# The last down pieces by token blocks, with the transposes inside, in a two-layer diffusion backbone

## Time and profile before

| | us |
|---|---|
| median of 3 runs (1637.95 to 1641.86) | 1638.42 |
| the profiled execution | 1642.74 |
| its span | 1641.2 |
| busy: TensorE, VectorE, ScalarE | 1598.5, 1124.8, 933.4 |
| mean granted clock of TensorE | 0.991 |

### The profile page before, as it was taken

The page is one execution under the profiler, slowest core; times in us unless marked ns, Lnnn a source line. Parts: engine busy times, 40 slices in busy tenths (PEclk is TensorE's granted clock), DMA queues, the critical chain, the costliest instruction groups (busy, mean ns, idle before and its releaser), DMA issues.

```text
span 1641.2 us, 22638 instructions
## 1 busy us (share of the span) xinstructions
PE 1598.5 (97%) x8278; PEld 1301.2 (79%) x8278; DVE 1124.8 (69%) x1478; ACT 933.4 (57%) x1347; POOL 48.8 (3%) x70
## 2 busy tenths in 40 slices
PE   7999999999999999899989999999999999999997
PEld 3886588988888887689678888888888888888885
DVE  5444533657553333543758999999999999899997
ACT  4415433622221322632667787787877787777875
POOL 0000000400000000000101000000000000000000
PEclk9999999999999999999999999999999999999999
DMA  8622732797442322542246999999999999999982
GB/s 345 216 77 103 308 127 85 264 363 239 165 169 103 116 90 103 194 182 77 65 177 269 421 420 420 382 400 379 374 388 361 391 370 401 362 393 376 372 334 73
DMA packets 68730, 428.88 MB, mean 261 GB/s; under 512 B 8880, under 2 KB 12720, under 8 KB 20656
## 3 DMA queue, kind: packets, MB, share of 16 engines
q1 hardware_dynamic: 60000, 396.93, 62.5%
q0 software_dynamic: 8656, 30.96, 5.1%
HBM read 404.25 MB, written 23.61 MB: 261 GB/s over the span
## 4 chain that ended last, share of the span: by engine, by line
PE 91%; DVE 4%; ACT 3%; DMA 1%; issue 1%; SPq 0%; DVEq 0%; ACTq 0%
PE ps L2027 28%; PE ps L2029 27%; PE ps L2028 27%; PE ps L2089 1%; PE ps L2045 1%; PE ps L2596 1%; DMA raw<-in_w 1%; DVE small L1452 1%; PE ps L2265 1%; PE ps L2286 1%; DVE raw L1668 1%; DVE wl L1198 0%; DVE raw L1667 0%; PE ps L2558 0%; PE ps L2290 0%
## 5 line engine op out<-in xcount | busy, mean ns | idle before, releaser
L1840 DVE TENSOR_TENSOR wl<-raw,wh 128x1024 fp32r<-128x1024 f32 x522 | 615.3, 1222 | 59.2 <-ACT wh L1099 52.2
L1099 ACT ACTIVATE wh<-raw 128x1024 fp32r<-128x1024 f32 x522 | 524.8, 1057 | 93.0 <-PE ps L2029 93.0
L2027 PE MATMUL ps<-wh,ah 128*128 128x512 f32 (+1 forms) x864 | 330.1, 382 | 0.5
L2029 PE MATMUL ps<-wh,al 128*128 128x512 f32 (+1 forms) x864 | 321.2, 372 | 0.0
L2028 PE MATMUL ps<-wl,ah 128*128 128x512 f32 (+1 forms) x864 | 320.5, 371 | 0.0
L2027 PE MATMUL ps<-ah,wh 128*128 128x512 f32 (+1 forms) x802 | 290.0, 362 | 6.6 <-DVE al L1228 4.7
L2029 PE MATMUL ps<-ah,wl 128*128 128x512 f32 (+1 forms) x802 | 282.2, 352 | 0.0
L2028 PE MATMUL ps<-al,wh 128*128 128x512 f32 (+1 forms) x802 | 282.1, 352 | 0.0
L2027 PE MATMUL ps<-wh,sh 128*128 128x512 f32 x536 | 209.9, 392 | 1.5 <-DVE sl L1557 1.5
L2029 PE MATMUL ps<-wh,sl 128*128 128x512 f32 x536 | 209.1, 390 | 0.0
L2028 PE MATMUL ps<-wl,sh 128*128 128x512 f32 x536 | 208.5, 389 | 0.0
(11 more groups left out here) (314 smaller groups left out, 1221.5 us busy)
## 6 DMA issues: line engine op xcount, KB each, us to landing
raw<-in_w SPq DMA_DIRECT2D x372, 1024.0 KB, 6.8
sent<-raw POOLq DMA_DIRECT2D x16, 512.0 KB, 24.5
back<-raw POOLq DMA_DIRECT2D x16, 512.0 KB, 25.2
x<-sent POOLq DMA_DIRECT2D x7, 512.0 KB, 11.0
back<-x POOLq DMA_DIRECT2D x7, 512.0 KB
x<-in_x SPq DMA_DIRECT2D x2, 1024.0 KB, 8.9
raw<-in_ukv SPq DMA_DIRECT2D x1, 1024.0 KB, 7.9
ah<-flat_rows POOLq DMA_DIRECT2D x2, 512.0 KB, 6.4
```

Of the source, the lines that this page charges most:

```text
L1099: act.activation(wh[:, J % SPLITS, piece_half(h)], slot(J % SLOTS)[:, piece_half(h)], ACT.Copy).then_inc(w_hi, 1)
L1840: ins = dve.tensor_tensor(wl[:, J % SPLITS, piece_half(h)], slot(J % SLOTS)[:, piece_half(h)], wh[:, J % SPLITS, piece_half(h)].bitcast(F3 ...
L2027: pe.matmul(out, lh, rh, start=start, stop=False)
L2029: return pe.matmul(out, ll, rh, start=False, stop=stop)
```

## The change

The hidden chunks 18 to 21 (four, before two) run by blocks of tokens. Chunks 20 and 21 are kept in `ah` and `al`, chunks 0 and 1, which are free then. The first two pairs of transposes stand inside block 3, between its chunks 19 and 20. Of the eight turned chunks, VectorE now makes 2, 3, 6 and 7 (in four buffers), ScalarE the others. Modulation pieces 40 and 41 move into piece 0, to chunk 3, and 42, 43 and 44 to chunks 4, 5 and 6. The split of OIN's piece 1, the squares of block 3 and the copy of modulation rows (`rows(10)`) come after the turned chunks on ScalarE, and the split after the gates of block 3 on VectorE. Both squares of a block run one behind the other, and the gate passes follow them. At the attention's end, the last head sum moves behind the four units of the Fourier chunks in the first token piece, and the roots of the first two sums come one unit and a half earlier. The diff, cut to its core:

```diff
@@ views
+        turned_at = lambda k: tmp[k % 2][:, 0:TL] if k // 2 % 2 == 0 else area(8704 + k % 2 * TL, TL)
+        late = NF - 2
+        hid_hi = lambda f: sh[:, f % 2, :] if f < late else ah[:, f - late, :]
+        hid_lo = lambda f: sl[:, f % 2, :] if f < late else al[:, f - late, :]
@@ scalar
             def hidden_hi(f):
-                if f >= 2:
+                if 2 <= f < late:
...
-            for d in range(NF // 2):
+            for d in range(NF // 2 - 1):
                 split(M_DOWN + d + 2)
                 if d + 1 < NF // 2:
                     hidden_hi(2 * d + 2)
                     hidden_hi(2 * d + 3)
...
-                    act.activation(junk[:, 0:512], ps[:, b, :], ACT.Square, accum_out=y_ss[:, t, 0:1]).then_inc(sem("row_sq"), 1)
-                    act.wait_ge(sem("y2_gated"), 2 * t + 1)
-                    act.activation(junk[:, 512:1024], ps[:, b + 1, :], ACT.Square, accum_out=y_ss[:, t, 1:2]).then_inc(sem("row_sq"), 1)
+                    for c in range(2):
+                        act.activation(junk[:, c * 512:(c + 1) * 512], ps[:, b + c, :], ACT.Square, accum_out=y_ss[:, t, c:c + 1]
+                                       ).then_inc(sem("row_sq"), 1)
...
             row_square("y", 2)
             for k in range(KD):
-                turned_chunk(k)
-                if k == 1:
-                    row_square("y", 3)
-                if k == 4:
-                    rows(10)
+                if k // 2 % 2 == 0:
+                    turned_chunk(k)
+                turned_hi(k)
+            split(M_OIN + 1)
+            row_square("y", 3)
+            rows(10)
             row_root("y", 2)
...
                 if u % 4 == 1 and u > 4:
                     head_squares(u // 4 - 1)
+                if u == len(ounits) - 3:
+                    head_ln(0)
+                    head_exp(0)
+                    head_ln(1)
                 if u == len(ounits) - 2:
-                    head_root(0, 1)
+                    head_exp(1)
...
             for h in range(DH):
-                if h == 2:
-                    head_root(DH // 2 - 1)
+                if h == 3:
+                    head_ln(2)
+                    head_exp(2)
@@ vector
-            for d in range(NF // 2):
+            for d in range(NF // 2 - 1):
...
-                for c in (1, 0):
-                    if c == 0:
-                        dve.wait_ge(sem("row_sq"), 2 * t + 1)
+                for c in range(2):
+                    dve.wait_ge(sem("row_sq"), 2 * t + c + 1)
...
             new_rows(1)
-            gated_rows(2)
             scaled(0)
             scaled(1)
+            gated_rows(2)
+            for k in range(0, KD, 4):
+                turned_chunk(k + 2)
+                turned_low(k)
+                turned_chunk(k + 3)
+                for n in range(1, 4):
+                    turned_low(k + n)
             gated_rows(3)
-            for k in range(KD):
-                low(N_O1L, k)
+            split(M_OIN + 1)
             new_rows(2)
             new_rows(3)
             split(M_OIN + 2)
@@ tensor
                 order = [(t, k) for k in (6, 7, 0, 1, 2, 3, 4, 5) for t in range(2)] if p == 0 else [(t, k) for t in range(2) for k in range(KD)]
                 for n, (t, k) in enumerate(order):
+                    if p == 0 and n == 4:
+                        head_sums(DH // 2 - 1)
...
-            for f in range(NF - 2):
+            for f in range(NF - 4):
...
             pe.wait_ge(w_lo, M_DOWN + NF // 2)
             pe.wait_ge(sem("hid_lo"), NF)
-            for t in range(ROW_BLOCKS):
-                for f in (NF - 2, NF - 1):
-                    mm = down_rows(f, t)
-                mm.then_inc(sem("y2_ps") if t < ROW_BLOCKS - 1 else w_used, 1)
...
+            for t in range(ROW_BLOCKS):
+                for f in range(NF - 4, NF):
+                    if (t, f) == (ROW_BLOCKS - 1, NF - 2):
+                        pe.wait_ge(sem("tok_made"), 2)
+                        for j in range(2):
+                            turn_pair(N_O1L, j)
+                    mm = down_rows(f, t)
+                    if (t, f) == (ROW_BLOCKS - 1, NF - 3):
+                        mm.then_inc(w_used, 1)
+                mm.then_inc(sem("y2_ps") if t < ROW_BLOCKS - 1 else w_used, 1)
             pe.wait_ge(sem("row_sq"), 2)
             pe.wait_ge(sem("y2_gated"), 2)
-            mod_piece(GAP_MODS)
-            mod_piece(GAP_MODS + 1)
-            pe.wait_ge(sem("tok_made"), 2)
-            for j in range(2):
-                turn_pair(N_O1L, j)
...
             def latent_chunk(k):
-                if k in (2, 4):
-                    pe.wait_ge(mod_h, MOD_H_BEFORE[N_O1L] + k)
-                    turn_pair(N_O1L, k // 2 + 1)
+                if k == 1:
+                    pe.wait_ge(mod_h, MOD_H_BEFORE[N_O1L] + 2)
+                    turn_pair(N_O1L, 2)
+                if k == 2:
+                    pe.wait_ge(sem("turned_dve"), 2)
+                    turn_pair(N_O1L, 3)
+                for n in {3: (0, 1), 4: (2,), 5: (3,), 6: (4,)}.get(k, ()):
+                    mod_piece(GAP_MODS + n)
                 pe.wait_ge(mod_lo, MOD_BEFORE[N_O1L] + k + 1)
-                if k in (1, 3, 5):
-                    filler(GAP_MODS + 2 + k // 2)
...
             for p in range(OIN):
+                if p == 1:
+                    pe.wait_ge(sem("y2_gated"), 2 * ROW_BLOCKS)
...
-            pe.wait_ge(sem("diff_out"), len(ounits))
-            head_sums(DH // 2 - 1)
             for p in range(4):
                 token_piece(p)
```

More of the change, by code:

```diff
@@ L177 @@
 MOD_BEFORE = {N_E1: 0, N_E2L: KD, N_E2C: 2 * KD, N_O1L: 3 * KD, N_O1C: 4 * KD}
-MOD_H_BEFORE = {N_E2L: KD, N_E2C: 2 * KD, N_O1L: 3 * KD, N_O1C: 4 * KD}
+MOD_H_BEFORE = {N_E2L: KD, N_E2C: 2 * KD, N_O1L: 3 * KD, N_O1C: 3 * KD + KD // 2}
 def cols_of(n):
@@ L850, in hidden_hi @@
                 act.wait_ge(evac_dve, evacs(hidden_evac(f), "dve"))
-                act.activation(sh[:, f % 2, :], hid[:, f, :], ACT.Copy).then_inc(sem("hid_hi"), 1)
+                act.activation(hid_hi(f), hid[:, f, :], ACT.Copy).then_inc(sem("hid_hi"), 1)
             for m in range(3, NF):
@@ L901, in row_root, with turned_bank, turned_hi @@
                 act.activation(col, col, ACT.Exp, scale=-0.5).then_inc(sem("row_root"), 1)
+            def turned_bank(k):
+                return ps[:, 4 + k // 2 % 2, (k % 2) * TL:(k % 2 + 1) * TL]
             def turned_chunk(k):
                 act.wait_ge(sem("tok_ps"), pair_ps(N_O1L, k // 2))
[L906 to L912, removed]
+                if k >= 4:
+                    act.wait_ge(mod_lo, MOD_BEFORE[N_O1L] + k - 3)
+                act.activation(turned_at(k), turned_bank(k), ACT.Identity, bias=mod1[:, k, 0:1], scale=scl[:, 1, 0, k, 0:1]).then_inc(mod_h, 1)
+                act.wait_ge(mod_h, MOD_H_BEFORE[N_O1L] + 2 * (k // 4) + k % 2 + 1)
+            def turned_hi(k):
+                if k // 2 % 2:
+                    act.wait_ge(sem("turned_dve"), 2 * (k // 4) + k % 2 + 1)
+                act.activation(ah[:, k, 0:TL], turned_at(k), ACT.Copy).then_inc(mod_hi, 1)
             def context_hi(k):
@@ L1004, in head_squares, with head_ln, head_exp @@
                 act.activation(two_heads(o_sq, n), two_heads(o_o, n), ACT.Square).then_inc(sem("osq_ready"), 1)
[L1006 to L1014, removed]
+            def head_ln(n):
+                act.wait_ge(sem("ossq_done"), n + 1)
+                act.activation(two_heads(o_rinv, n), ps[:, HEAD_SUMS[n], :], ACT.Ln, bias=eps[:, 0:1], scale=1.0 / P
+                               ).then_inc(sem("oln"), 1)
+            def head_exp(n):
+                act.wait_ge(sem("oln"), n + 1)
+                act.activation(two_heads(o_rinv, n), two_heads(o_rinv, n), ACT.Exp, scale=-0.5).then_inc(sem("oroot"), 1)
             attention("diff", ounits, exp_o, out_o, last_piece)
@@ L1556, in hidden_lo @@
                 dve.wait_ge(sem("hid_hi"), f + 1)
-                dve.tensor_tensor(sl[:, f % 2, :], hid[:, f, :], sh[:, f % 2, :].bitcast(F32), ALU.subtract
+                dve.tensor_tensor(hid_lo(f), hid[:, f, :], hid_hi(f).bitcast(F32), ALU.subtract
                                   ).then_inc(sem("hid_lo"), 1)
@@ L1605, in scaled, with turned_chunk, turned_low @@
                                   ).then_inc(sem("tok_made"), 1)
+            def turned_chunk(k):
+                dve.wait_ge(sem("tok_ps"), pair_ps(N_O1L, k // 2))
+                if k >= 4:
+                    dve.wait_ge(mod_lo, MOD_BEFORE[N_O1L] + k - 3)
+                dve.tensor_scalar(turned_at(k), ps[:, 4 + k // 2 % 2, (k % 2) * TL:(k % 2 + 1) * TL],
+                                  scl[:, 1, 0, k, 0:1], mod1[:, k, 0:1], ALU.mult, ALU.add).then_inc(sem("turned_dve"), 1)
+            def turned_low(k):
+                dve.wait_ge(mod_hi, MOD_BEFORE[N_O1L] + k + 1)
+                dve.tensor_tensor(al[:, k, 0:TL], turned_at(k), ah[:, k, 0:TL].bitcast(F32), ALU.subtract).then_inc(mod_lo, 1)
```

(9 more changed lines are left out.)

## The result

The changed kernel takes 1654.97 us (median of 4 runs, 1652.61 to 1656.47) against 1638.59: a ratio of 1.009, 95% interval 1.0076 to 1.0104, so 16.4 us slower. Its profiled execution took 1656.47 us, span 1654.8, against 1642.74 and 1641.2: 13.7 us more.

A forecast was written before the change was run, and what follows sets the result against it. The prediction took TensorE's gaps and clock to bound the kernel. 10.4 us lost up to modulation 46 less 3.1 gained at the attention's end gave +7.3; with 0.8 more on the median 1638.42 this made 1646.5 us, range 1641 to 1651.

The forecast's parts named there:

- The wait ahead of the blocks: Before the last four hidden chunks, TensorE idles 5.35 us: a loss of 3.8, plus 2.4 for the low clock.
- Piece 0 starts without a wait: Second layer's first projection: TensorE starts piece 0 at the down product's end, where before it waited 3.29 us.
- The split moved past a queue: Inside piece 0, OIN piece 1's split ends at E + 10.5, modulation 42 lands at E + 15.3, TensorE stands 9.7 us.
- part 3: From piece 0 to modulation 46: the late split delays the fetches, so 46 starts at 707.3, 10.4 us later.
- it lands near 25.4; 1.8 idle: Modulation 45, fetched behind OIN's piece 2 in turns of 2.6 us, lands near E + 25.4; TensorE idles 1.8.
- now 46 is early enough, 7.46: From modulation 45's start to 46's: 7.46 us, where the kernel before took 8.05 with 0.59 idle.
- the low clock through the broken piece: Rival, chance 0.10: the low clock stays through piece 0's alternating work and waits, 4.5 us more, 1651.
- Part 4: Attention's end: head sums behind the Fourier chunks, first token piece ends 3.1 us earlier, bounds 1.0 and 4.2.
- I added 0.8: Added to the median 1638.42 because quicker runs may partly lack the low-clock stretches removed; half of the 1.7 us.
- the covered case: Bound of the fetch term: with the fetch covered entirely, piece 0 ends at E + 11.9, modulation 46 starts 2.5 us earlier.

The follow-up runs named there:

- Taking its cause out: Changed kernel with hidden chunks 20 and 21 split ahead of 18 and 19, all four ahead of the split of OIN's piece 0: 1.0041 of the kernel before.
- all causes out: Changed kernel with hidden chunks 20 and 21 first, OIN piece 1's split ahead of all turned chunks, modulation 45 behind piece 1: 0.9961 and 0.9965 of before in two runs.
- the kernel with TensorE kept busy: Changed kernel with modulation 45 behind piece 1, plus 19 unread matmuls in the gap before modulation 42: 1.0052 of the kernel before.
- Part 4 alone: The kernel before with only the head-sum edits of the diff: 0.998 of the kernel before, some 3.3 us faster.
- The three causes: Taken out of the changed kernel singly: hidden chunks 20 and 21 first, 1.0041; OIN piece 1's split between turned chunks 3 and 4, 1.0031; modulation 45 behind piece 1, 1.0058.
- the kernel with separate buffers: The kernel before with the head-sum edits and hidden chunks 20 and 21 kept in ah and al: 0.9974 of the kernel before.

## Why the prediction was half right

The direction and the chain of causes were right; the size was too small: +8 forecast, +16.4 measured, outside the range, which ended at 1651.

- *The wait ahead of the blocks.* 5.35 forecast, 5.36 in the trace; resumed at 649.15 against 649.32, and the down product's end E at 674.4 in both. Taking its cause out gave 8 us, uncertain by some 3, where 3.8 + 2.4 = 6.2 were booked.
- *Piece 0 starts without a wait.* Right.
- *The split moved past a queue.* Issue at E + 10.5 forecast, E + 10.4 measured (684.80); landing 4.7 us later; the gap 9.7 against 9.19. Moving the split gave back 9.7 us, uncertain by some 3.
- *The step that failed* is in the sum of part 3: "it lands near 25.4; 1.8 idle" for modulation 45, and behind it "now 46 is early enough, 7.46". I gave each queued fetch a turn of 2.6 us, from the one pair in the earlier trace rows. With several under way, 44 landed 10.4 us after its issue at 685.6 (at 696.0, 1.1 later than forecast), OIN 2 after 7.0 (698.6) and 45 after 7.5 (702.5): 6.5 us for the last two, 3.2 each. So 45 started at 702.55 and not at 699.8 (2.8 us). The wait for 45 was 3.80 us, and that brought the clock down a third time: from 45 to 46 it took 10.26 and not 7.46 (2.8 us). Together 5.5 of the 8.3 us that were missed. The trace of before had shown that 2.6 isn't the turn of every queued fetch: the piece that SyncE issued at 698.16, behind three other fetches (1.6 MB) in the 1.3 us before, landed 9.2 us later. The forecast named this as a rival, the low clock through the broken piece, with 0.10 and 4.5 us; it came true in part, through piece 1 and not through piece 0, and should have had the larger share. The Trainium skill's section on HAM oscillation (TensorE: Matmul & The Clock Gate) says that bursts between waits for data start at the low clock each time. The trace agrees for the waits of 9.19 and 3.80 us on the DMA (0.50 in the windows), and the wait of 5.36 on VectorE did the same; waits of 1.20 and 1.99 us in the first run with all causes out left the clock whole. The section counts half of the low stretch as lost. Behind 45 this stretch lasts until about 709.0, 6.4 us, so half would be 3.2, and 2.8 is near it: matmuls of 256 columns go from 0.12 to 0.21 us apart there, not to 0.24. In piece 0, however, the kernel with TensorE kept busy shows a price near nothing.
- *Part 4.* 3.1 forecast. In the changed kernel's trace the first transposes of the next stage come 12.4 us late (870.88 against 858.45), 15.9 less 12.4 = 3.5; alone it gave 3.3. The working lets TensorE go on at 828.05, where 830.31 less 2.53 is 827.78, which leaves the size as it is.
- *The rest.* On the profiled execution: 7.3 forecast, + 5.5, - 0.4 for part 4, + 1.5 for a longer low stretch in the token stage (10.2 us against 6.8 by the windows; the experts start 13.9 late). Part 4 alone has 3.4 there, so its length isn't the same in every execution. Then - 0.3 after that: 13.6, the spans' difference.
- *From the profiled execution to the median* I added 0.8. The medians differ by 16.4 and the profiled executions by 13.7, so it was 2.7. The kernel before alone spread from 1636.46 to 1645.92 over 20 runs, so one profiled execution fixes the middle no better than that, and the remaining 1.9 us lie within that spread; no run shows a cause for them.
- *Slips in the working.* By its own terms 45 lands at E + 25.7 and not 25.4 (20.5 and two turns of 2.6), and the covered case ends at E + 11.5 and not 11.9. Neither changes the verdict.

The three causes in the changed kernel gave 8.0, 9.7 and 5.2 us one by one, 22.9 in sum, and 21 together. That fits causes which simply add up, but doesn't show it: each of these differences is uncertain by 3 to 4 us, the three lean on the same 1.009, and the kernel with all three out has the split at another place than the one that moved it alone.

## What to carry to other kernels

When a step is moved later on its engine, follow what its completion frees: here a split of 2 us sat in nobody's way, but the slot that it freed was the next fetch's, and the queue behind that is in order. When several buffers are waited for at once, the wait costs the latest of them, and here separate buffers gained nothing while their fill stayed queued behind other work. When a wait on a fetch is taken out, count the fetches in the stretch: if they follow one another with little slack, the wait can move to the next one. And before two traces are compared by their times, take off what stands ahead of the stretch, and remember that one execution is one draw: the same kernel took 55.7 and 60.0 us over the same stretch.

## What the runs showed that I had not expected

- Fetches of 1 MB that overlap don't keep the pace of the first ones. In the changed kernel 42 landed at 689.5 and 43 at 692.1, 2.6 us apart, with 420 GB/s in the window from 688; 44 came 3.9 later, OIN 2 2.6 later and 45 3.9 later. In the windows from 692 to 708 the queue moved 309 to 358 GB/s with a DMA share of 0.81 to 1.00, and the pieces issued from 691.5 on landed 7.0 us and more after issue, where 42 took 4.7. Why nearly the same share moved less is open; it wasn't tried.
- A gap of 3.80 us brought the clock down when it had been whole for less than 7 us (from 695.3 to 702.1 by the shares of the windows), one of 2.44 us did so in the kernel with separate buffers, and 1.54 us never did in any of these traces. Between them it is open: in the kernel with all causes out the clock held behind a wait of 1.99 us in one execution and fell behind one of 1.91 in the other. Keeping the clock whole through the 9.2 us gap brought nothing, since what came next waited for data anyway.
